# Weights in half tiles: a smaller unit for the weight stream of a float32 network

## The reference, cut to what matters

```python
for layer in range(4):
    x = x + 0.5 * swiglu(rms_norm(x), ffn1_w_gu[layer], ffn1_w_down[layer])     # 1024 -> 2*2816 -> 1024
    x = x + mixer(rms_norm(x))       # layer 0, 3: gated linear attention; 1: windowed attention; 2: latent attention
    x = x + 0.5 * swiglu(rms_norm(x), ffn2_w_gu[layer], ffn2_w_down[layer])
x = layer_norm(ALPHA * x + rg_lru_block(x))
x = layer_norm(ALPHA * x + conv_ffn(x))          # 1024 -> 2*3072, causal convolution of 3 taps, gelu(a)*b -> 1024
x = layer_norm(ALPHA * x + stick_breaking_attention(x) @ w_out)
x = layer_norm(ALPHA * x + conv_ffn(x))
```

## Time and profile before

| what | value |
|---|---|
| median of three runs | 3272.21 us (3271.46 to 3274.34) |
| profiled execution, its own time | 3273.65 us |
| its span, first to last instruction | 3271.8 us |
| TensorE matmul busy | 2948.0 us, 90% |
| VectorE / ScalarE / GpSimd busy | 2020.8 / 1367.7 / 313.7 us |
| mean granted TensorE clock | 0.953 |
| weight stream (SyncE's queue) | 467.30 MB, 43.0% of 16 engines |

### The profile page before, as it was taken

How to read it: one execution, slowest core, us unless ns; L and a number is a source line. 1 busy time by engine, 2 the same in 40 slices (tenths; PEclk the granted TensorE clock), 3 DMA queues, 4 the chain that set the end, 5 groups by cost and what they waited for, 6 DMA issues and landing times.

```text
span 3271.8 us, 44866 instructions
## 1 busy us (share of the span) xinstructions
PE 2948.0 (90%) x19567; PEld 2679.1 (82%) x19567; DVE 2020.8 (62%) x2245; ACT 1367.7 (42%) x1430; POOL 313.7 (10%) x391
## 2 busy tenths in 40 slices
PE   6997779999988999999899999786999798796987
PEld 6997769999976999985499999786899698694986
DVE  5557775555657656543655555777556666747666
ACT  4444434444444444433544344443444433343433
POOL 0005430000002000000000000544000100000000
PEclk9998989999989999999899999898999799897998
DMA  5543325565531655532146455332454444441443
GB/s 188 192 156 106 98 80 168 193 193 196 165 129 39 206 193 168 193 107 82 52 156 204 152 199 178 116 101 80 153 195 142 159 151 155 141 159 61 160 170 108
DMA packets 362056, 478.12 MB, mean 146 GB/s; under 512 B 9226, under 2 KB 324324, under 8 KB 361860
## 3 DMA queue, kind: packets, MB, share of 16 engines
q1 hardware_dynamic: 358448, 467.30, 43.0%
q0 software_dynamic: 1776, 6.77, 0.7%
q10 hardware_dynamic: 1636, 1.18, 0.1%
HBM read 474.17 MB, written 1.05 MB: 145 GB/s over the span
## 4 chain that ended last, share of the span: by engine, by line
PE 65%; DVE 20%; ACT 7%; DMA 5%; issue 3%; ACTq 0%; SPq 0%; DVEq 0%
PE Wk L547 12%; PE Wk L548 12%; PE Wk L549 12%; PE Y L547 7%; PE Y L548 7%; PE Y L549 7%; DVE w_lo L1470 6%; ACT w_hi L1061 4%; DMA ring<-in_ffn_w_up 3%; DVE work L1693 2%; PE Wk L555 1%; DVE work L1603 1%; DVE work L1599 1%; DVE work L1696 1%; PE Y L857 1%
## 5 line engine op out<-in xcount | busy, mean ns | idle before, releaser
L1470 DVE TENSOR_TENSOR w_lo<-ring,w_hi 128x2048 fp32r<-128x2048 f32 x436 | 1002.4, 2306 | 757.3 <-ACT w_hi L1061 717.1
L547 PE MATMUL Wk<-xT_hi,w_hi 128*128 128x256 f32 x4320 | 1235.5, 286 | 33.4 <-DVE xT_lo L1502 18.4
L548 PE MATMUL Wk<-xT_lo,w_hi 128*128 128x256 f32 x4320 | 1228.1, 284 | 0.0
L549 PE MATMUL Wk<-xT_hi,w_lo 128*128 128x256 f32 x4320 | 1227.7, 284 | 0.0
L1061 ACT ACTIVATE w_hi<-ring 128x2048 fp32r<-128x2048 f32 x436 | 828.7, 1907 | 693.1 <-DMA ring<-in_ffn_w_gu 257.7
L547 PEld LDWEIGHTS Wk<-xT_hi,w_hi 128*128 128x128 f32 x4320 | 835.3, 193 | 43.1 <-issue 23.3
L548 PEld LDWEIGHTS Wk<-xT_lo,w_hi 128*128 128x128 f32 x4320 | 835.1, 193 | 4.6 <-issue 0.9
L549 PEld LDWEIGHTS Wk<-xT_hi,w_lo 128*128 128x128 f32 x4320 | 834.6, 193 | 0.0
L547 PE MATMUL Y<-w_hi,hid_hi 128*128 128x512 f32 x896 | 358.6, 400 | 48.7 <-DVE w_lo L1470 31.6
L548 PE MATMUL Y<-w_lo,hid_hi 128*128 128x512 f32 x896 | 354.3, 395 | 0.0
L549 PE MATMUL Y<-w_hi,hid_lo 128*128 128x512 f32 x896 | 353.2, 394 | 0.0
(11 more groups left out here) (250 smaller groups left out, 3046.4 us busy)
## 6 DMA issues: line engine op xcount, KB each, us to landing
ring<-in_ffn_w_gu SPq DMA_DIRECT2D x176, 1024.0 KB, 5.1
ring<-in_ffn_w_down SPq DMA_DIRECT2D x112, 1024.0 KB, 5.0
ring<-in_ffn_w_up SPq DMA_DIRECT2D x48, 1024.0 KB, 5.2
ring<-in_hg_w_in SPq DMA_DIRECT2D x40, 1024.0 KB, 5.1
ring<-in_na_w_in SPq DMA_DIRECT2D x12, 1024.0 KB, 5.2
ring<-in_hg_w_out SPq DMA_DIRECT2D x8, 1024.0 KB, 4.9
ring<-in_lru_w_in SPq DMA_DIRECT2D x8, 1024.0 KB, 5.5
ring<-in_kv_w SPq DMA_DIRECT2D x8, 1024.0 KB, 5.5
```

Source lines behind the costliest of these rows:

```text
L547: pe.matmul(o, l_hi, r_hi, start=first, stop=False)
L548: pe.matmul(o, l_hi, r_lo, start=False, stop=False)
L549: return pe.matmul(o, l_lo, r_hi, start=False, stop=last)
L1470: dve.tensor_tensor(lo, raw(t), hi.bitcast(F32), ALU.subtract).then_inc(lo_done, 1)
```

## The change: what it does, and the diff

Every tile becomes two units of 128 x 1024, (t, 0) and (t, 1). A tile of 8 row blocks is cut by rows; a down or output tile is cut by its 1024 columns. The raw ring has six half slots and the split ring seven: 3 and 3.5 tiles instead of 2 and 4, in the same memory. Units are loaded, split and released in the order of `units_of`: at feature-wise joints the halves of two neighbouring tiles alternate. `unit_done` replaces `tile_done`. Products run half by half, so TensorE can start on the first half and releases it first. At the end of lru and stick, `last_by_tokens` gets the last two tiles together and signals their four units at once, at the very end. The set-up moves: the transposes and copies of parameters go between chunks 0 and 1 of sublayer 0, `set_up` behind chunk 4. Matmuls, operands and bytes are the same.

```diff
-RAW, SPLIT = 2, 4
-SLOT = 2048
+RAW, SPLIT = 6, 7
+HALF = 1024
+SET_UP_AT = 4
+    def units_of(s):
+        t0, t1 = base[s], end[s]
+        order = [(t, h) for t in range(t0, t1) for h in range(2)]
+        if s == 0 or not by_tokens(s - 1):
+            order[0:4] = [(t0, 0), (t0 + 1, 0), (t0, 1), (t0 + 1, 1)]
+        if subs[s][0] in ("ffn", "na", "mla"):
+            order[-4:] = [(t1 - 2, 0), (t1 - 1, 0), (t1 - 2, 1), (t1 - 1, 1)]
+        return order
...
-                old = t - RAW
-                if old in nth:
-                    sp.wait_ge(lo_done, nth[old] + 1)
-                elif old >= 0:
-                    sp.wait_ge(tile_done, old + 1)
-                sp.dma_start(slot(t, n, w), src).then_inc(raw_in[t % RAW], 16)
+                i = pos[u] - RAW
+                if i >= 0 and units[i] in nth:
+                    sp.wait_ge(lo_done, nth[units[i]] + 1)
+                elif i >= 0:
+                    sp.wait_ge(unit_done, i + 1)
+                n, w = src.shape[1:]
+                sp.dma_start(raw(u, n * w).rearrange("p (k n) -> p k n", k=n), src).then_inc(raw_use(u)[0], 16)
...
             def f_product(t, o):
-                hi, lo = weights(t)
-                for f in range(2):
-                    for k in range(KD):
-                        ...
-                mm.then_inc(tile_done, 1)
+                for h in range(2):
+                    weights((t, h))
+                    for f in range(2):
+                        mm = f_part((t, h), o, f)
+                    mm.then_inc(unit_done, 1)
...
+            def y_half(a, n, first=False):
+                weights((a[0], n))
+                for tt in range(TT):
+                    mm = y_part_of(*a, tt, n, first=first)
+                mm.then_inc(unit_done, 1)
+            def last_half(a, n):
+                weights((a[0], n))
+                y_part_of(*a, 0, n, last=True).then_inc(y_part, 1)
+                y_part_of(*a, 1, n, last=True).then_inc(unit_done, 1)
             def t_product(t, l_hi, l_lo, first=False):
+                for n in range(2):
+                    y_half((t, l_hi, l_lo), n, first)
+            def last_pair(s, a, b, b_ready):
+                y_half(a, 0)
+                b_ready()
+                last_half(b, 0)
+                y_half(a, 1)
+                turn(s + 1, 0)
+                turn(s + 1, 1)
+                last_half(b, 1)
+            def last_by_tokens(tiles, ready):
+                for tt in range(TT):
+                    for i, a in enumerate(tiles):
+                        if tt == 0:
+                            ready[i]()
+                        for n in range(2):
+                            if tt == 0:
+                                weights((a[0], n))
+                            mm = y_part_of(*a, tt, n, last=i == len(tiles) - 1)
+                            if tt == 0 and i == len(tiles) - 1:
+                                mm.then_inc(y_part, 1)
+                mm.then_inc(unit_done, 2 * len(tiles))
...
-            def high(t):
-                n = nth[t]
-                act.wait_ge(raw_in[t % RAW], use(t))
+            def high(u):
+                n = nth[u]
+                act.wait_ge(*raw_use(u))
                 if n >= SPLIT:
-                    act.wait_ge(tile_done, split_tiles[n - SPLIT] + 1)
-                act.activation(split_of(t)[0], raw(t), ACT.Copy).then_inc(hi_done, 1)
+                    act.wait_ge(unit_done, pos[split_units[n - SPLIT]] + 1)
+                act.activation(split_of(u)[0], raw(u), ACT.Copy).then_inc(hi_done, 1)
             def splits(upto):
-                while nxt[0] < len(split_tiles) and split_tiles[nxt[0]] <= upto:
+                while nxt[0] < len(split_units) and split_units[nxt[0]][0] <= upto:
...
                     rest(j, j % 2, g)
                     if j:
                         splits(g + 5)
+                    if s == 0 and j == SET_UP_AT:
+                        act.preload_act_table_set("natural_log_exp_and_others")
+                        set_up()
...
                 for j in range(1, chunks - 1):
                     gate_up(t0 + 3 * j - 1, j % 2)
                     pe.wait_ge(hidden_ready, n0 + j)
+                    if s == 0 and j == 1:
+                        first_parameters()
                     t_product(t0 + 3 * j + 1, *hid(j - 1), first=j == 1)
+                    if s == 0 and j == 1:
+                        pe.wait_ge(par_ready, 7)
```

More of the change, by code:

```diff
@@ L106, in build, with by_tokens, units_to @@
     end = [base[s] + TILES[subs[s][0]] for s in range(NS)]
-    split_tiles = [base[s] + j for s in range(NS) for j in range(TILES[subs[s][0]])
-                   if j not in AS_FLOAT32.get(subs[s][0], ())]
-    nth = {t: n for n, t in enumerate(split_tiles)}
+    def by_tokens(s):
+        return subs[s][0] in ("lru", "cffn", "stick")
+    def units_of(s):
[6 more added lines that the diff above has]
+        return order
+    units = [u for s in range(NS) for u in units_of(s)]
+    pos = {u: i for i, u in enumerate(units)}
+    as_float32 = {base[s] + j for s in range(NS) for j in AS_FLOAT32.get(subs[s][0], ())}
+    split_units = [u for u in units if u[0] not in as_float32]
+    nth = {u: n for n, u in enumerate(split_units)}
+    def units_to(n):
+        return max(pos[(n - 1, 0)], pos[(n - 1, 1)]) + 1
     with ExitStack() as ctx:
@@ L320, in vs_before, with raw, raw_use, split_of @@
             return before(s, {"na": 8, "mla": 4, "stick": 12})
[L322 to L335, removed]
+        def raw(u, size=HALF):
+            return ring[:, pos[u] % RAW, 0:size]
+        def raw_use(u):
+            return raw_in[pos[u] % RAW], 16 * (pos[u] // RAW + 1)
+        def split_of(u):
+            return w_hi[:, nth[u] % SPLIT, :], w_lo[:, nth[u] % SPLIT, :]
+        def raw_rows(t, n, w):
+            return [raw((t, h), n // 2 * w).rearrange("p (k n) -> p k n", k=n // 2)[:, k, :]
+                    for h in range(2) for k in range(n // 2)]
         def f_src(w, c0, n):
@@ L341, in t_src, with ffn_tiles @@
             return w[r0:r0 + 256, :].rearrange("(k p) n -> p k n", p=P)
+        def ffn_tiles(gu, down, chunks, F):
+            for j in range(chunks + 1):
+                if j < chunks:
+                    yield f_src(gu, j * 256, 256), 8, 256
+                    yield f_src(gu, F + j * 256, 256), 8, 256
+                if j:
+                    yield t_src(down, 256 * (j - 1)), 2, D
         def tiles_of(kind, idx, layer):
@@ L624, in last_tile @@
[L624 to L629, removed]
-                if not by_tokens(s):
-                    turn(s + 1, 0)
-                    turn(s + 1, 1)
-                y_block(*a, *order[3], last=True).then_inc(tile_done, 1)
+            def y_half(a, n, first=False):
+                weights((a[0], n))
+                for tt in range(TT):
+                    mm = y_part_of(*a, tt, n, first=first)
+                mm.then_inc(unit_done, 1)
@@ L1464, in _, with low @@
             nxt = [0]
[L1466 to L1470 removed]
+            def low(u):
+                dve.wait_ge(hi_done, nth[u] + 1)
+                hi, lo = split_of(u)
+                dve.tensor_tensor(lo, raw(u), hi.bitcast(F32), ALU.subtract).then_inc(lo_done, 1)
             def splits(upto):
[L1474 to L1475 removed]
+                while nxt[0] < len(split_units) and split_units[nxt[0]][0] <= upto:
+                    low(split_units[nxt[0]])
                     nxt[0] += 1
```

235 lines of the change are left out of this document (102 added, 133 removed).

## The result

| | before | after |
|---|---|---|
| median of the runs, us | 3273.28 (3271.46 to 3275.6, 4 runs) | 3187.6 (3186.87 to 3188.41, 4 runs) |
| the profiled execution, us (span) | 3273.65 (3271.8) | 3187.94 (3186.1) |
| mean granted clock | 0.953 | 0.957 |

The ratio is 0.9738, 95% interval 0.9721 to 0.9755: 85.7 us faster. The forecast was 3195 us, in a range of 3175 to 3232.

A forecast was written before the change was run, and what follows sets the result against it. TensorE was taken to bound the ffn, while other stages had waits and lower-clock stretches. The terms summed to -76.9 us from the profiled 3273.65, giving 3196.7 and a median of 3195 us, range 3175 to 3232.

The forecast's parts named there:

- two cffn: Both cffn: loads land early, the round falls under TensorE's 17.2 us per chunk; 33.8 and 19.9 us saved, together 53.7.
- start: First ffn: with the set-up moved, TensorE's 5.1 us wait for r_row and 2.3 us of low clock go; -7.4 us.
- hg, two: Both hg: low parts start earlier in 10 places and the ring is deeper, less 3.8 us for added instructions; -7 us.
- na: Before the softmax: one half instead of a tile lies ahead of the first scores, and one more such place; -3 us.
- mla: Two loads of w_out tiles in the chain of mla get partly or nearly wholly hidden; -6 us.
- lru without its LayerNorm: Waits for two loads in lru shrink, partly limited by TensorE's products; -5 us.
- stick without its LayerNorm: A load of 4.75 us in stick's chain shrinks, while VectorE has three tiles to split there; -4 us.
- LayerNorm behind lru and stick: A split ahead of the LayerNorm waits for the last units, signalled only at the end; +5.1 us each, +10.2.
- other joints, ffn: Joints between other stages give about -1 us; the seven ffn were put at cost 0.
- Rival 1: Only cffn and start gain, hg, na, mla, lru and stick give nothing net, LayerNorm loss stays: 3221 us; chance 16%.
- rival 2: In the cffn another wait replaces the load's, so half of 53.7 us stays: 3222 us; chance 9%.
- Rival 4: In every ffn and cffn chunk, half loads at 4.0 us each become the bound, 24 us against 17.2: 4030 us; chance 5%.

The follow-up runs named there:

- e4: The kernel after the change, with the set-up and the turning of parameters back at their old place behind the first product of the first ffn: 3195.64 us.
- e9: The kernel after the change, unchanged, timed again as the measure for a repeat run beside it: 3187.01 us, ratio 0.9732.
- e3: The kernel after the change, with VectorE and ScalarE taking one split unit pair less before the LayerNorm behind lru and stick: 3176.93 us, ratio 0.9707.
- e1: The kernel after the change, with four raw and eight split half slots instead of six and seven: 3185.41 us, ratio 0.973.
- e2: The kernel before the change, with four raw and three split whole-tile slots instead of two and four: 3367.95 us, ratio 1.0286.
- e6: The kernel after the change, with each high and low part of a half in two instructions of 512 columns instead of one of 1024: 3198.68 us.
- e5: The kernel after the change, with every half loaded by two DMAs of 256 KB instead of one of 512 KB: 3188.44 us, ratio 0.9736.
- e7: The kernel after the change, with a product starting only when both halves of its tile are split: 3192.3 us, ratio 0.9745.
- e8: The kernel of e3 a second time, beside e9 on the same chip: 3178.28 us, ratio 0.9703.

## Why the prediction was right, point by point

The mechanism held. The miss is 8.8 us in the profiled executions (-76.9 forecast, -85.7 measured); most terms gave more than forecast, na, mla and lru less, and the LayerNorm cost more. That the total came so near is in part luck, since the working of hg did not hold.

| term | forecast | measured | from |
|---|---|---|---|
| two cffn | -33.8, -19.9 | -36.2, -19.9 | table of stages |
| start | -7.4 | -9.7 | table of stages; 7.6 of it the move (e4) |
| hg, two | -7 | -9.4 | table of stages (-11.2 with e9) |
| na | -3 | -1.6 | table of stages (-2.9 with e9) |
| mla | -6 | -5.3 | table of stages |
| lru without its LayerNorm | -5 | -3.4 | e3: 106.8 - 110.2 |
| stick without its LayerNorm | -4 | -5.6 | e3: 157.5 - 163.1 |
| LayerNorm behind lru and stick | +10.2 | +11.0 | e3: 5.1 + 5.9 |
| other joints, ffn | -1 | -5.3 | table of stages |

*The cffn.* The round without the load is under 17.2 us, TensorE bounds, and the last chunk keeps one wait: 2.2 us against 2.4. The idle time that went is 26.0 us (37.3 - 11.3) against 25.8. The rest of the miss is clock: of the 13.3 us of surplus I had left 5, and 3.2 were left. What the forecast got right for an incomplete reason is which part of the change does it. It named the depth; e1 and e2 show that halves alone (221.7 and 214.9 us) and depth alone (227.2 and 217.1) both break the loop; in both TensorE no longer waits for w_lo, as when the round is under its own. Their gains do not add up.

*The ffn* stayed at 189.0 us: the seven slots, the added instructions (e6) and the doubled loads (e5) cost nothing there. The seven ffn behind the first gained 5.3 us where I wrote 1 for all joints. This step failed by size: I had compared only a middle stage, and "seven look like this one" was not so, as one took 190.5 us and one 191.0. The one that was 191.0 us before is 189.0 now; its chain of waits held a load of w_down of 6.34 us at 1860.93, near its entry. e7 puts 2.2 of the 5.3 us on the half by half walk; the rest I did not separate.

*Start.* The terms 5.1 + 2.3 measured 7.0 to 7.6. The miss is the two microseconds that came on top with the other parts of the change; no run separates these.

*hg.* The sum was near, its working was not. I had counted ten places of 0.87 us, three head pairs and the entry. The places lie elsewhere: in the first hg ScalarE's square of the first head pair comes 3.5 us nearer to the stage's beginning than before (102.6 us after it, against 106.1), the later three pairs add 0.4, 0.1 and 0, and the way from the last pair to the next stage 1.2. TensorE's one wait for a low part in each hg, 2.7 us before, is gone. e7 says that the walk is the smaller part: taking it away costs 2 to 4 us, not 8.7, and the first square still comes at 102.9. Nor is it the depth of the raw ring, for e1 has 264.6 and 263.8 us, at most 2 more. In the first hg TensorE's idle time fell by only 2.1 us (57.5 to 55.4); the rest is that it ran less at the lower clock (busy for 212.1 us before, 209.0 after, with the same matmuls). What brings the first pair forward stays open. The term for added instructions, +3.8 for 48 tiles cut in two, was somewhat high: e6 adds twice as many for 4.8 to 6.6 us, which makes some 2.4 to 3.3.

*na* gave 1.6 to 2.9 of 3 us, *lru* 3.4 of 5, *stick* 5.6 of 4. *mla* gave 5.3 of 6, and e1 shows its cause: with four raw half slots the two loads of w_out are in the chain, with six they are not.

*The LayerNorm* is the step in which the change loses, and it was read from the order of the program alone: the wait of TensorE for x grew from 6.3 us to 11.4 at each entry, 5.1 each as forecast. Taking the loss away gives 8.7 us (e8 against e9) and not the whole 11.0, as the first cffn gets 2.3 longer.

*The rivals.* Rival 1 (nothing from hg, na, mla, lru, stick) and rival 2 (another wait in the cffn) are not seen. Rival 4 (the loads become the bound) is refuted by the ffn at 189.0 us, and again by e5: even twice as many loads change nothing. Its price of 4.0 us per load, one behind the other, took the time from issue to landing for the time per load; the halves show 4.5 us to landing, and the ffn runs six of them in 17.2 us all the same.

## What to carry to other kernels

Follow a slow chunk around once, through the load, each engine and back to the slot it frees, and compare the round with the bounding engine: any edit that brings it under is enough, a second one adds little (at most 6 us of 36 here). Cutting the unit of a ring in half is a way to buy depth without memory, and costs only where the splitting engines hold the chain. When a ring gets shallower in units of work, look at the joints and not at the steady loop: whatever is issued ahead of the work that ends a stage delays it by a whole wait.

## What was not expected of the hardware

The time of a load from issue to landing falls slowly with its size: for the gate and up weights of the ffn 5.1 us for 1 MB, 4.5 for 512 KB, 3.2 for 256 KB; for those of the cffn 5.2, 6.0 and 5.1, so there half the size brought nothing. An added split instruction in e6 cost 0.09 us of engine time where 0.15 to 0.19 was worked out from instructions standing alone. Those that follow one another overlap: on VectorE 1744 of 0.708 us would be 1234.8 us, and it was busy for 1138.1.
